# Last mixer of a two-block model: conv sums of three channel tiles in PSUM, the first tile on Pool, two weight units converted there

## What is computed

```python
u = rms_norm(h, mix_norm_g)
proj = u @ w_in                                   # 1024 -> 2560
q, k, v, glu_a, glu_g = jnp.split(proj, splits, axis=-1)
attn_out = moba_attention(heads(q), heads(k), heads(v), rel_bias)      # 8 heads of 64
# conformer_conv, 512 channels:
c = glu_a * sigmoid(glu_g)
c = causal_depthwise_conv(c, w_dw) + b_dw          # 31 taps for each channel
c = silu(layer_norm(c) * ln_g + ln_b)
h = h + concat([attn_out, c]) @ w_out
h = h + (silu(rms_norm(h) @ w_gate) * (rms_norm(h) @ w_up)) @ w_down
return rms_norm(h, final_norm_g)
```

## Time and profile before

| | us |
|---|---|
| median of 3 runs | 1941.03 |
| lowest and highest | 1939.72, 1941.93 |
| time of the profiled execution | 1939.78 |
| its span by the profile | 1937.6 |
| granted clock of TensorE, mean of the span | 0.971 |
| busy: TensorE, VectorE, ScalarE, Pool | 1841.1, 1380.6, 1109.4, 70.1 |

### The profile page before, as it was taken

One profiled execution on the slowest core, in us unless ns is written; L12 is line 12 of the kernel. 1 busy time (PEld: TensorE's weight loads), 2 busy tenths in 40 slices (PEclk: granted clock), 3 DMA queues, 4 the chain that ended last, 5 costly groups with the idle time before them and its releaser, 6 DMA issues.

```text
span 1937.6 us, 26159 instructions
## 1 busy us (share of the span) xinstructions
PE 1841.1 (95%) x10199; PEld 1569.4 (81%) x10199; DVE 1380.6 (71%) x1216; ACT 1109.4 (57%) x1028; POOL 70.1 (4%) x54
## 2 busy tenths in 40 slices
PE   8998999899889999999999999999999968879998
PEld 7897999788768878888788788887887857769997
DVE  3655545634568888888888887888888877965454
ACT  4543443345447677777676777777777743433433
POOL 0001000100200000000000000000000001220000
PEclk9998999899989999999999999999999989889999
DMA  9824555533559999999899999998999972325551
GB/s 270 294 88 153 174 190 179 173 110 108 165 170 363 346 327 369 339 335 368 311 366 340 333 371 329 345 368 306 368 343 332 372 251 77 109 98 174 184 185 44
DMA packets 252147, 490.47 MB, mean 253 GB/s; under 512 B 14172, under 2 KB 96645, under 8 KB 251710
## 3 DMA queue, kind: packets, MB, share of 16 engines
q1 hardware_dynamic: 248000, 474.67, 70.3%
q0 software_dynamic: 3184, 14.29, 2.3%
q10 hardware_dynamic: 910, 0.76, 0.1%
HBM read 488.61 MB, written 5.80 MB: 255 GB/s over the span
## 4 chain that ended last, share of the span: by engine, by line
PE 88%; DVE 8%; ACT 2%; issue 2%; DMA 0%; DVEq 0%; ACTq 0%
PE psum L543 26%; PE psum L545 26%; PE psum L546 26%; DVE ta L2025 2%; PE psum L981 2%; PE psum L1053 2%; PE psum L1027 1%; PE psum L631 1%; PE psum L662 1%; DVE wl L1565 1%; ACT wh L1173 1%; DVE u L1965 1%; PE psum L604 1%; DVE small L1610 1%; DVE x L1622 0%
## 5 line engine op out<-in xcount | busy, mean ns | idle before, releaser
L1565 DVE TENSOR_TENSOR wl<-ring,wh 128x2048 fp32r<-128x2048 f32 x442 | 1012.7, 2291 | 355.9 <-ACT wh L1173 355.2
L1173 ACT ACTIVATE wh<-ring 128x2048 fp32r<-128x2048 f32 x450 | 862.1, 1916 | 418.3 <-PE psum L543 349.6
L543 PE MATMUL psum<-wh,xTh 128*128 128x512 f32 (+1 forms) x1136 | 437.0, 385 | 7.9 <-DVE wl L1565 5.4
L545 PE MATMUL psum<-wl,xTh 128*128 128x512 f32 (+1 forms) x1136 | 426.6, 376 | 0.0
L546 PE MATMUL psum<-wh,xTl 128*128 128x512 f32 (+1 forms) x1136 | 426.6, 376 | 0.0
L543 PE MATMUL psum<-xTh,wh 128*128 128x256 f32 x1088 | 313.6, 288 | 6.5 <-ACT gnat L1413 1.9
L545 PE MATMUL psum<-xTl,wh 128*128 128x256 f32 x1088 | 310.6, 285 | 0.0
L546 PE MATMUL psum<-xTh,wl 128*128 128x256 f32 x1088 | 310.4, 285 | 0.0
L543 PE MATMUL psum<-wh,wnh 128*128 128x512 f32 x672 | 267.0, 397 | 0.0
L545 PE MATMUL psum<-wl,wnh 128*128 128x512 f32 x672 | 264.6, 394 | 0.0
L546 PE MATMUL psum<-wh,wnl 128*128 128x512 f32 x672 | 264.0, 393 | 0.0
(11 more groups left out here) (262 smaller groups left out, 1170.9 us busy)
## 6 DMA issues: line engine op xcount, KB each, us to landing
ring<-in_w_moe SPq DMA_DIRECT2D x336, 1024.0 KB, 5.2
ring<-in_w_dense SPq DMA_DIRECT2D x33, 1024.0 KB, 5.2
ring<-in_w_in_ab SPq DMA_DIRECT2D x14, 1024.0 KB, 10.8
ring<-in_w_in_cd SPq DMA_DIRECT2D x12, 1024.0 KB, 5.3
ring<-in_w_gate SPq DMA_DIRECT2D x11, 1024.0 KB, 5.3
ring<-in_w_up SPq DMA_DIRECT2D x11, 1024.0 KB, 5.3
ring<-in_w_down SPq DMA_DIRECT2D x11, 1024.0 KB, 4.9
ring<-in_w_in SPq DMA_DIRECT2D x10, 1024.0 KB, 5.7
```

Source lines behind the costliest of these rows:

```text
L543: last = pe.matmul(o, a[0], b_[0], start=first, stop=False)
L545: pe.matmul(o, a[0], b_[1], start=False, stop=False)
L1173: act.activation(upper_half[i], ring[:, u_, :], ACT.Copy).then_inc(hi_ready[s_], 1)
L1565: dve.tensor_tensor(lower_half[i], ring[:, u_, :], upper_half[i].bitcast(F32), ALU.subtract)\
```

## The change

- **Sums in PSUM.** The conv sums of tile 1 stand in bank 5 and those of tiles 2 and 3 in bank 4. The last tap of tile 1 (index 30), and for tiles 2 and 3 the tap with index 23 and all behind it, write `ta` in SBUF (`CONV_MOVED`). Before `out_unit(0)`, which uses banks 4 and 5, TensorE waits for a new semaphore `conv_moved`, which VectorE raises after gap 14.
- **Tile 0 on Pool.** VectorE does the taps of tiles 1, 2, 3 only (93 taps). Pool, once `glu(0)` is done, does for each of the 31 taps a product (`upad` times the weight, broadcast along the tokens, into one of four pieces of `nw`) and an add (into `ta`), 62 `tensor_tensor` on 128x256. The product of the next tap is issued ahead of the add of this one. After the last add Pool raises `conv_first`, on which TensorE waits behind `conv_done`.
- **Units.** Pool writes the lower halves of n = 6 (v1) and n = 7 (the first unit of `w_out`), after its taps. VectorE takes n = 2, 4 and 8 and gives up n = 7.
- **Order of the taps.** `B2_TAPS` is written anew: tile 1 alone in the first gaps (24 calls of one tap), then 7 calls of three tiles, then 24 calls of two.

```diff
-POOL_LOWERS = (2, 4, 6)
-B2_TAPS = {**{i: [(0, 1)] * 3 for i in range(4)}, **{i: [(0, 1, 2, 3)] * 2 for i in (4, 5, 6, 7, 12, 13)},
-           **{i: [(0, 1, 2, 3), (2, 3)] for i in (8, 9, 10, 11, 14)}, 15: [(2, 3)] * 2, 16: [(2, 3)] * 2, 17: [(2, 3)] * 5}
+POOL_LOWERS = (6, 7)
+CONV_MOVED = [0, 30, 23, 23]
+FIRST_TILE = 1
+B2_TAPS = {**{i: [(1,)] * 5 for i in range(4)}, 4: [(2, 3, 1)] * 2, 5: [(2, 3, 1)] * 2, 6: [(2, 3, 1)] * 2, 7: [(2, 3, 1), (2, 3)],
+           8: [(2, 3)] * 2, 9: [(2, 3)] * 2, 10: [(2, 3)] * 2, 11: [(2, 3)] * 3, 12: [(2, 3)] * 3, 13: [(2, 3)] * 3,
+           14: [(2, 3)] * 2, 15: [(2, 3)] * 2, 16: [(2, 3)] * 2, 17: [(2, 3)] * 2}
@@ tensor engine
             pe.wait_ge(step_evac, steps[0])
+            pe.wait_ge(conv_moved, 1)
             out_unit(0, 9, lambda: b2_gap(16))
...
             pe.wait_ge(conv_done, 1)
+            pe.wait_ge(conv_first, 1)
@@ vector engine
+            def summed(c, j):
+
+                if j >= CONV_MOVED[c]:
+                    return ta[:, c, :]
+                return bank[5 - c // 2][:, c % 2 * T:(c % 2 + 1) * T]
...
-                        last = dve.scalar_tensor_tensor(ta[:, c, :], upad[:, c, j:j + T], cw[:, c, j:j + 1], ta[:, c, :],
+                        last = dve.scalar_tensor_tensor(summed(c, j), upad[:, c, j:j + T], cw[:, c, j:j + 1], summed(c, j - 1),
                                                         ALU.mult, ALU.add)
...
+                if i == 14:
+                    assert all(n > m for n, m in zip(tapped[FIRST_TILE:], CONV_MOVED[FIRST_TILE:]))
+                    dve.nop().then_inc(conv_moved, 1)
...
-            for _ in range(2):
-                taps(0, 1)
+            for _ in range(4):
+                taps(1)
...
-                if w - 1 in POOL_LOWERS or w == 9:
+                if w - 1 in POOL_LOWERS:
@@ pool engine
+            pool.wait_ge(step_evac, STEPS_GLU - 2)
+            pool.wait_ge(conv_in, 1)
+
+            products = nw.rearrange("p t n -> p (t n)").rearrange("p (j c) -> p j c", j=4)
+
+            def product(j):
+                pool.tensor_tensor(products[:, j % 4, :], upad[:, 0, j:j + T], cw[:, 0, j:j + 1].broadcast_to([P, T]), ALU.mult)\
+                    .then_inc(g_chain, 1)
+
+            product(0)
+            for j in range(CONV):
+                if j + 1 < CONV:
+                    product(j + 1)
+                more = cw[:, 0, 31:32].broadcast_to([P, T]) if j == 0 else ta[:, 0, :]
+                pool.wait_ge(g_chain, 1 if j == 0 else 2 * j + 1)
+                last = pool.tensor_tensor(ta[:, 0, :], products[:, j % 4, :], more, ALU.add)
+                if j + 1 < CONV:
+                    last.then_inc(g_chain, 1)
+                else:
+                    last.then_inc(conv_first, 1)
             for n in POOL_LOWERS:
                 lower(1, n)
-            lower(1, 8)
             rstd_tiles()
             lower(1, 11)
```

More of the change, by code:

```diff
@@ L352, in build @@
         moe_done = sem("moe_done")
+        conv_first = sem("first_channels_done")
+        conv_moved = sem("conv_sums_in_sbuf")
         conv_turned = sem("conv_transposed")
@@ L2022, in taps @@
                     if j == 0:
-                        last = dve.tensor_scalar(ta[:, c, :], upad[:, c, 0:T], cw[:, c, 0:1], cw[:, c, 31:32], ALU.mult, ALU.add)
+                        last = dve.tensor_scalar(summed(c, 0), upad[:, c, 0:T], cw[:, c, 0:1], cw[:, c, 31:32], ALU.mult, ALU.add)
                     else:
-                        last = dve.scalar_tensor_tensor(ta[:, c, :], upad[:, c, j:j + T], cw[:, c, j:j + 1], ta[:, c, :],
+                        last = dve.scalar_tensor_tensor(summed(c, j), upad[:, c, j:j + T], cw[:, c, j:j + 1], summed(c, j - 1),
                                                         ALU.mult, ALU.add)
@@ L2055, in _ @@
             b2_gap(17)
-            assert tapped == [CONV] * 4
+            assert tapped[1:] == [CONV] * 3
             dve.nop().then_inc(conv_done, 1)
```

## The result

| | before | changed |
|---|---|---|
| median | 1940.38 us (4 runs, 1939.22 to 1941.93) | 1957.98 us (4 runs, 1952.68 to 1958.16) |
| ratio to before, 95% interval | | 1.0084 (1.0065 to 1.0102) |
| span of the profiled execution | 1937.6 | 1956.4 |

The change makes the kernel 0.8% slower by the ratio (the interval excludes no change), and 17.6 us slower by the medians. A gain of 10.4 was forecast; the time lies outside the range, and on the other side.

What follows compares the result with a forecast made beforehand. VectorE bounds the stage before; after the change Pool's chain does, with the conv tiles' turns at 1656.4 + 62t, 1699.8 at t = 0.70, 10.4 us earlier. Predicted median 1930.6 us, range 1922.5 to 1944.

Steps and rivals of the forecast that it cites:

- What bounds the kernel: Stretch 1617.3 to 1708.3: VectorE bounds it, busy 86.0 of 91.0 us, 13.8 of it stalls beside Pool's conversions.
- Part 1, sums in PSUM: VectorE's taps with PSUM sums: no stalls beside Pool, no extra price; VectorE through at 1691.3, 17 us earlier.
- Rival 5: Taps writing PSUM still stall beside Pool; turns of the conv tiles at 1728.3, +18, 1959 us; chance 0.03.
- The wait of a lower half for Pool: VectorE's five lower halves beside Pool each wait half of a 0.7 us Pool instruction, 1.8 us in all.
- Part 2, t: Pool's chain becomes the bound: 62 operations on 128x256, each taking t = 0.70 us, ending at 1673.5.
- 1656.4 + 62t: Start of the conv tiles' turns, with t the time per Pool operation: 1699.8 at 0.70, against 1710.17 before.
- the 2.5 us for a slow clock: Around v1: TensorE, having stood some 5 us, runs the next 6 us at clock 0.54, costing 2.5 us.
- the sum of 21.7: From v1's start to the conv tiles' first turn: v1, first w_out unit, attention, last heads, slow clock; 21.7 us.
- The nearer bound of the prediction: For t: 0.91 us per 128x256 Pool operation, worked out from power operations on 128x8 and 128x1.
- behind the turns all is as before: After the turning of the conv tiles nothing changes, so no time is gained or lost there.

Runs made afterwards that it cites:

- one wait in four taps: The changed kernel, but after every fourth tap Pool waits until all it has issued is done, products still issued one ahead: 1922.40 us, ratio 0.9918.
- the two mended kernels: The changed kernel with Pool waiting twice, or once, in every four taps: 1921.46 us and 1922.40 us.
- two waits in four taps: The changed kernel, but Pool pauses before and after the add of every fourth tap, with no product issued ahead there: 1921.46 us, ratio 0.9917.

## Why the prediction was wrong, point by point

**What bounds the kernel: right.** The sum by stage, not the share of the whole span, told where VectorE's time counts. With the hold taken away the stage falls from 94.3 to 77.2.

**Part 1, sums in PSUM: right.** The price was set to zero. VectorE's taps with sums in PSUM in the changed kernel (one tile's instructions; shortest/median/longest in ns, first and last start):

```profile
L2038 DVE SCALAR_TENSOR_TENSOR psum<-gA,cw,psum x73: 476/490/491, 1621.0 to 1708.9; 128x256 f32<-128x256 f32 x73
```

Because of the hold only some 14 of these lie beside Pool's chain. With one wait in four taps Pool's chain runs from 1615.1 to 1665.8, beside most of them:

```profile
L2038 DVE SCALAR_TENSOR_TENSOR psum<-gA,cw,psum x73: 476/490/490, 1615.6 to 1674.3; 128x256 f32<-128x256 f32 x73
```

490 ns against 480 in SBUF, and the longest of either 73 is 491: none is stretched. A call of one costs 0.523 (6.79/13), as forecast. By the rule that was cited from the Trainium skill, "VectorE: DVE Perf Modes", section "The TRN2 errata — SBUF-src ops pay a fixed extra latency per instruction", an estimate makes a tap 65 ns dearer; the trace disagrees, and the measured 10 decide. Rival 5 falls with the same row.

**The wait of a lower half for Pool: the step that failed.** "Half of 0.7 for each of five, 1.8" supposed that VectorE gets the port at the end of the Pool instruction in hand. The first of the five waited 30.7, and by its end Pool's chain was all but over, so the others waited for nothing. In the kernels that pause at every fourth tap or oftener the term was about right: each of the five waited 0.0 to 0.6 us.

**Part 2, t (the time of one Pool operation of 128x256): right in kind, too high in size.** From start to start a product takes 0.57 us and an add 0.70, 0.635 on the mean where 0.70 was taken. 62 x 0.635 = 39.4 in 1656.4 + 62t puts the turns 14.4 earlier. The stages of the two mended kernels are 16.2 and 17.1 shorter than before; there TensorE stood only 2.0 and 1.7 us before v1, so the 2.5 us for a slow clock in the sum of 21.7 were not due, which makes 16.9. Without them the sum has 19.2 from v1's lower half to the first turn of the conv tiles; with one wait in four taps it took 19.7 (1670.4 to 1690.1). So the sum holds once the hold is gone.
## What to carry to other kernels

Where Pool runs a chain of queued instructions beside VectorE work with two SBUF inputs, let it wait on its own semaphore every few instructions (here after eight, 5.1 us; a wait costs about 0.1 us), and don't spread the requests of VectorE too thin: freeing VectorE's taps from the port starved its next conversion here. In the profile look at the longest single instruction of each form, not at busy time, since waiting for the port counts as busy. And don't take evidence for one direction of a hand-over as evidence for the other.

## What the runs showed of the hardware

**The hold.** VectorE was kept off by about 48 Pool instructions in a row; with instructions of 256 columns the turn lies between 5.5 and 7.3 us of unbroken run (both outcomes at 6.2), 9 to 11 instructions.

**Small Pool instructions.** 128x256: product with a broadcast column 0.57 us, sum of two tensors 0.68 to 0.70, start to start; 128x128 0.39 on the mean. The nearer bound of the prediction, worked out from a power, was a bad neighbour; the proportion of the conversion (0.57) was the good one.

**A first tap to PSUM.** A multiplication of 128x256 by a column takes 0.55 us into PSUM (VectorE's timeline of the changed kernel, 1620.42), where the same into SBUF took 0.41 in the kernel before, and the taps that follow it 0.49; it occurs once a tile.

**TensorE's clock in the tail.** The tail is 18.5 to 18.6 us in six of the profiled executions and 20.0 to 21.4 in the other eight, though the program is the same there. In it TensorE waits for the `silu` ahead of the turning of the conv output, in the changed kernel

```profile
PE psum L720 <- ACT u L1538: 2.0, 1, 2.0
```

and with two waits in four taps:

```profile
PE psum L720 <- ACT u L1538: 1.4, 1, 1.4
```

The busy times of the 13 us that follow, in the changed kernel and then in the other (columns as above):

```profile
1736.00:1749.00 13.00, 11.93 (x45) 9.51 (x43) 3.64 (x4) 4.80 (x4) 0.50 (x1) 0.74 0.27 88
```

```profile
1698.00:1711.00 13.00, 10.53 (x50) 8.37 (x49) 5.18 (x6) 5.93 (x6) 0.79 (x1) 1.00 0.45 162
```

In the changed kernel the granted clock behind the wait was 0.74, a mean between the levels of 1.2 and 2.4 GHz; in the other it was 1.00. All executions with a wait of 2.0 have the longer tail, all with 0.9 to 1.4 the shorter. But the shorter wait isn't the cause. The turning of the conv tiles, just ahead of the tail, in the changed kernel and then in the other:

```profile
1726.20 1.04 PE L1141 MATMUL psum<-ident,ta 128*128 128x128 f32 x8
```

```profile
1690.60 1.91 PE L1141 MATMUL psum<-ident,ta 128*128 128x128 f32 x8
```

The eight turns take 1.04 us in all eight executions with the long tail and 1.91 or 1.92 in the six others, the kernel before among them. There the low clock comes earlier: in the three us ahead of the tail and the three behind its start it was 0.67 and 0.77 with two waits in four taps, and 1.00 and 1.00 in the changed kernel. TensorE then has its matmuls done later and stands less for the `silu`, which comes at the same time in both (VectorE's next conversion starts 11.53 us into the tail in both), so the low clock costs nothing there. Where it comes only behind the wait, the matmuls that follow pay for it, and that is the 2.7 us. Why it comes early in some executions and late in others stays open; there is one trace of each kernel, so it isn't shown that this belongs to the kernel. The prediction had "behind the turns all is as before"; in the profiled executions that term was off by these 2.7 us.
